# Splitting the first projections by tile and moving the last tiles' norm transposes behind their first pieces

## The reference

```python
xn = rms_norm(x, lp['norm_mix'])
proj = xn @ lp['w_in']                      # q | k | v | pool_in | two gates
q = rms_norm(q per head); k = rms_norm(k per head)
a = sliding-window attention (own 64-frame chunk and the two before, ALiBi bias, sink logit)
pl = pooling mixer: trailing means over 2/4/8/16 frames minus the frame, per-group map, scale
mix = (sigmoid(g0) * (a @ w_br_attn) + sigmoid(g1) * (pl @ w_br_pool)) @ w_out
x = x + mix
h = rms_norm(x, lp['norm_ffn']) @ lp['w_up']            # width 2 * 2816
hc = causal depthwise conv of width 3 over h
x = x + (gelu(gate half of hc) * value half of hc) @ w_down
```

## Time and profile before

| | |
|---|---|
| median of the timed runs | 4879.23 us (2 runs, 4861.53 and 4896.93) |
| profiled execution | 4373.59 us |
| its span, first to last instruction of the slowest core | 4372.1 us |
| spans of the 8 cores | 4332.4 to 4372.1 us |
| mean granted TensorE clock of the cores | 0.931 to 0.942 |
| TensorE, VectorE, ScalarE, GpSimd busy | 86%, 60%, 42%, 15% |

### The profile page before, as it was taken

One profiled execution on the slowest core, in us unless ns is written; L12 is line 12 of the kernel. 1 busy time (PEld: TensorE's weight loads), 2 busy tenths in 40 slices (PEclk: granted clock), 3 DMA queues, 4 the chain that ended last, 5 costly groups with the idle time before them and its releaser, 6 DMA issues.

```text
span 4372.1 us, 64992 instructions; the slowest of 8 cores (4332.4 to 4372.1 us)
## 1 busy us (share of the span) xinstructions
PE 3781.1 (86%) x21100; PEld 1882.6 (43%) x21100; DVE 2609.7 (60%) x4570; ACT 1837.1 (42%) x3723; POOL 640.3 (15%) x682
## 2 busy tenths in 40 slices
PE   3776479898898989898989989898989898989989
PEld 1434234443444444444444444444444444444444
DVE  2464547557474747566564746474757566574647
ACT  2333234344444535354444444353445344444443
POOL 1000000000121202020212112121202020211112
PEclk9877688899999999999999999999999999999999
DMA  7999967486333343343433433334334342443333
GB/s 132 196 195 180 192 152 206 117 184 181 130 134 114 130 150 131 105 145 126 158 105 138 139 138 124 121 139 145 122 117 146 125 154 96 149 127 138 114 125 120
DMA packets 104076, 616.74 MB, mean 141 GB/s; under 512 B 13600, under 2 KB 17728, under 8 KB 42304
## 3 DMA queue, kind: packets, MB, share of 16 engines
q1 hardware_dynamic: 88368, 528.69, 35.3%
q0 software_dynamic: 15376, 83.89, 12.7%
HBM read 621.11 MB, written 75.55 MB: 159 GB/s over the span
## 4 chain that ended last, share of the span: by engine, by line
PE 69%; DVE 14%; DMA 7%; issue 5%; ACT 4%; POOL 1%; DVEq 0%; SPq 0%; ACTq 0%; POOLq 0%
PE psb L885 27%; PE psb L940 13%; PE psb L790 11%; DVE srt L502 7%; DMA wslot<-wun 5%; PE psb L845 4%; PE psb L795 3%; PE psb L799 3%; PE psb L535 2%; PE psb L707 1%; ACT xh L453 1%; PE psb L713 1%; DMA wsc<-wslot 1%; PE psb L472 1%; DVE xsl L826 1%
## 5 line engine op out<-in xcount | busy, mean ns | idle before, releaser
L885 PE MATMUL psb<-xnT,wslot 128*128 128x512 bf16 (+5 forms) x6624 | 1365.7, 372 | 76.9 <-DMA wslot<-wun 35.9
L885 PEld LDWEIGHTS psb<-xnT,wslot 128*128 128x128 bf16 x6624 | 655.3, 103 | 783.2 <-issue 172.9
L940 PE MATMUL psb<-wslot,actT 128*128 128x512 bf16 (+1 forms) x2992 | 671.7, 386 | 35.0 <-DMA wslot<-wun 32.8
L908 POOL TENSOR_TENSOR actT<-ug,uv 128x512 bf16<-128x512 f32 x308 | 391.8, 1272 | 1092.4 <-DVE uv L903 756.1
L906 ACT ACTIVATE ug<-ug 128x512 f32<-128x512 f32 (+2 forms) x396 | 238.8, 603 | 682.7 <-DVE ug L903 682.5
L790 PE MATMUL psb<-xnT,wslot 128*128 128x512 bf16 (+2 forms) x2304 | 511.9, 378 | 5.9 <-DMA wslot<-wun 5.9
L940 PEld LDWEIGHTS psb<-wslot,actT 128*128 128x128 bf16 (+1 forms) x2992 | 294.2, 99 | 398.6 <-issue 78.4
L808 DVE TENSOR_TENSOR s0b<-psb,s0b 128x512 f32<-128x512 f32 (+2 forms) x144 | 94.5, 656 | 576.3 <-PE psb L799 569.9
L826 DVE TENSOR_TENSOR xsl<-psb,xsl 128x512 f32<-128x512 f32 (+1 forms) x396 | 270.4, 689 | 269.6 <-PE psb L940 209.8
L453 ACT ACTIVATE xh<-xsl 128x1024 bf16<-128x1024 f32 (+1 forms) x141 | 148.6, 1054 | 622.5 <-DVE xsl L826 340.3
L502 DVE RECIPROCAL srt<-srt 128x512 f32<-128x512 f32 (+1 forms) x108 | 353.1, 3269 | 91.1 <-ACT srt L500 90.3
(11 more groups left out here) (135 smaller groups left out, 3912.2 us busy)
## 6 DMA issues: line engine op xcount, KB each, us to landing
wslot<-wsc SPq DMA_DIRECT2D x366, 1024.0 KB, 6.0
wslot<-wun POOLq DMA_DIRECT2D x66, 1024.0 KB, 28.3
wsc<-wslot SPq DMA_DIRECT2D x48, 1024.0 KB, 13.9
wslot<-wsc SPq DMA_DIRECT2D x72, 512.0 KB, 6.6
xsl<-xp SPq DMA_DIRECT2D x35, 512.0 KB, 4.5
yp<-xsl SPq DMA_DIRECT2D x32, 512.0 KB, 5.0
...
```

Source lines behind the costliest of these rows:

```text
L885: S.op("pe", lambda e, k=k, bk=bk, half=half, pi=pi, wuv=wuv, c0=c0, c1=c1: e.matmul(out=psb[bk][:, c0:c1], lhsT=wuv[:, k, half * 256 + pi ...
L908: S.op("dve" if grp in groups[:2] else "pool", lambda e, ub=ub, j=j: e.tensor_tensor(out=actT[:, j, C0:N], in0=ug[ub][:, C0:N], in1=uv[ub] ...
L940: S.op("pe", lambda e, kc=kc, bk=bk, cs=cs, n=n, wdv=wdv, cb=cb, k0=k0, k1=k1: e.matmul(out=psb[bk][0:n, 0:512], lhsT=actT[:, kc, cs], rhs ...
```

## The change

norm_post of some tiles is no longer called where it was but put into a list, defer_q, and called from within the next stage.

- stage_F puts the last two of (at most three) tiles, 2 and 3 in a group of four, into the list. stage_G takes four banks at its start, for both j of the first weight unit with both halves, and runs the columns in three splits: tiles 0 and 1 (256 columns) in all four banks, then the transposes and the copy of tile 2, tile 2's columns (128) in all four banks, the transposes and the copy of tile 3, tile 3's columns (128) in all four.
- The last tile's norm_post before stage_B is put into the list in both layers. k_job takes both banks at once and runs the 384 columns of K 0 and K 1, then the transposes and the copy of the last tile, then its 128 columns for K 0; then follows the head norm's square for K 0, and K 1's 128 columns with the flush of the sum matmul come in the second job.

```diff
--- before.py
+++ after.py
@@ -460,6 +460,11 @@
                  reads=[xr, f"rstd{ti}"], writes=[f"xh{b}"])
 
         post_done = set()
+        defer_q = []
+
+        def run_deferred():
+            while defer_q:
+                defer_q.pop(0)()
 
         def norm_post(l, ni, t, ti):
             post_done.add((t["T"], l, ni))
@@ -527,14 +532,33 @@
             wkv, wkvr = W.get(U_KV)
             wkvv = wkv[:, 0:3072].rearrange("p (k c) -> p k c", k=8)
             npr = grp["np"]
+            kbanks = {}
+
+            def k_mm(g, c0, c1, rr):
+                bk = kbanks[g]
+                for k in range(8):
+                    S.op("pe", lambda e, g=g, k=k, bk=bk, c0=c0, c1=c1: e.matmul(out=psb[bk][:, c0:c1], lhsT=wkvv[:, k, g * 128:(g + 1) * 128],
+                                                                   rhs=xnT[:, k, c0:c1], start=(k == 0), stop=(k == 7)),
+                         reads=[wkvr] + rr, writes=[f"ps{bk}"])
+
             def k_job(g):
-                bk = pbank()
                 csp = tiles[-1]["col"]
-                for (c0, c1, rr) in ((0, csp, xres[:-1]), (csp, N, xres[-1:])):
-                    for k in range(8):
-                        S.op("pe", lambda e, g=g, k=k, bk=bk, c0=c0, c1=c1: e.matmul(out=psb[bk][:, c0:c1], lhsT=wkvv[:, k, g * 128:(g + 1) * 128],
-                                                                       rhs=xnT[:, k, c0:c1], start=(k == 0), stop=(k == 7)),
-                             reads=[wkvr] + rr, writes=[f"ps{bk}"])
+                if g == 0:
+                    kbanks[0] = pbank(); kbanks[1] = pbank()
+                    if defer_q:
+                        kbanks["split"] = True
+                        k_mm(0, 0, csp, xres[:-1])
+                        k_mm(1, 0, csp, xres[:-1])
+                        run_deferred()
+                        k_mm(0, csp, N, xres[-1:])
+                    else:
+                        k_mm(0, 0, N, xres)
+                else:
+                    if kbanks.get("split"):
+                        k_mm(1, csp, N, xres[-1:])
+                    else:
+                        k_mm(1, 0, N, xres)
+                bk = kbanks[g]
                 dests = [(0, npr * 128, kTw[0:64, 2 * g, 0:npr * 128], f"kTw{g}", (0, 64)),
                          (0, npr * 128, kTw[64:128, 2 * g + 1, 0:npr * 128], f"kTw{g}", (64, 128))]
                 for t in tiles:
@@ -641,6 +665,22 @@
                 return 128 if l == 0 else 256
             return 0
 
+        def col_splits(grp, C0):
+            act = [(ti, t) for ti, t in enumerate(grp["tiles"]) if t["col"] >= C0]
+            N_ = grp["N"]
+            if len(act) >= 3:
+                parts = [act[:-2], act[-2:-1], act[-1:]]
+            elif len(act) == 2:
+                parts = [act[:1], act[1:]]
+            else:
+                parts = [act]
+            out = []
+            for pi_, p in enumerate(parts):
+                c0 = p[0][1]["col"]
+                c1 = parts[pi_ + 1][0][1]["col"] if pi_ + 1 < len(parts) else N_
+                out.append((c0, c1, [f"xnT{ti}" for ti, _ in p]))
+            return out
+
         def prev_of(l, t):
             if t["kind"] == "s":
                 return (kcache[l], [f"kcache{l}"]), (Vcache[l], f"Vcache{l}"), (pinhist[l], f"pinhist{l}")
@@ -848,7 +888,11 @@
                         resid_add(grp, t, bk, cb)
                     norm_pre(l, 1, t, ti)
                 if 0 <= si - 2 < nt_:
-                    norm_post(l, 1, sub[si - 2][1], sub[si - 2][0])
+                    ndef = min(3, nt_) - 1
+                    if si - 2 >= nt_ - ndef:
+                        defer_q.append(lambda l=l, t=sub[si - 2][1], ti2=sub[si - 2][0]: norm_post(l, 1, t, ti2))
+                    else:
+                        norm_post(l, 1, sub[si - 2][1], sub[si - 2][0])
             W.done(U_OUT)
             W.done(U_OUT + 1)
 
@@ -870,22 +914,37 @@
                      reads=[f"corr{hid}", "ctmp"], writes=[f"corr{hid}"])
                 S.op("pool", lambda e, hs=hs, cr=cr: e.tensor_tensor(out=cr[:, :, 1], in0=hs[:, :, 1], in1=cw0, op=ALU.mult),
                      reads=[hr, "pv"], writes=[f"corr{hid}"])
+            pre_banks = {}
             for f in range(11):
                 wu, wur = W.get(U_UP + f)
                 wuv = wu[:].rearrange("p (k c) -> p k c", k=8)
-                for pi in range(2):
-                    j = 2 * f + pi
-                    ub = j % 2
-                    for half, (c, ubuf, ures) in enumerate(((j, ug[ub], f"ug{ub}"), (22 + j, uv[ub], f"uv{ub}"))):
-                        bk = pbank()
-                        csp = grp["tiles"][-1]["col"]
-                        splits = ((C0, csp, xres[:-1]), (csp, N, xres[-1:])) if (j == 0 and csp > C0) else ((C0, N, xres),)
-                        for (c0, c1, rr) in splits:
+                if f == 0:
+                    for pi in range(2):
+                        for half in range(2):
+                            pre_banks[(pi, half)] = pbank()
+                    for (c0, c1, rr) in col_splits(grp, C0):
+                        for (pi, half), bk in pre_banks.items():
                             for k in range(8):
                                 S.op("pe", lambda e, k=k, bk=bk, half=half, pi=pi, wuv=wuv, c0=c0, c1=c1: e.matmul(
                                     out=psb[bk][:, c0:c1], lhsT=wuv[:, k, half * 256 + pi * 128: half * 256 + (pi + 1) * 128],
                                     rhs=xnT[:, k, c0:c1], start=(k == 0), stop=(k == 7)),
                                     reads=[wur] + rr, writes=[f"ps{bk}"])
+                        if defer_q:
+                            defer_q.pop(0)()
+                    run_deferred()
+                for pi in range(2):
+                    j = 2 * f + pi
+                    ub = j % 2
+                    for half, (c, ubuf, ures) in enumerate(((j, ug[ub], f"ug{ub}"), (22 + j, uv[ub], f"uv{ub}"))):
+                        if f == 0:
+                            bk = pre_banks[(pi, half)]
+                        else:
+                            bk = pbank()
+                            for k in range(8):
+                                S.op("pe", lambda e, k=k, bk=bk, half=half, pi=pi, wuv=wuv: e.matmul(
+                                    out=psb[bk][:, C0:N], lhsT=wuv[:, k, half * 256 + pi * 128: half * 256 + (pi + 1) * 128],
+                                    rhs=xnT[:, k, C0:N], start=(k == 0), stop=(k == 7)),
+                                    reads=[wur] + xres, writes=[f"ps{bk}"])
                         S.op("act", lambda e, bk=bk, c=c, ubuf=ubuf: e.activation(out=ubuf[:, C0:N], in_=psb[bk][:, C0:N], func=ACTF.Identity,
                                                                                  bias=pvc(l, OFF_CB + c, 1), scale=pvc(l, OFF_CW[2] + c, 1)),
                              reads=[f"ps{bk}", "pv"], writes=[ures])
@@ -985,7 +1044,10 @@
                         norm_pre(l, 0, t, ti)
                 for ti, t in enumerate(grp["tiles"]):
                     if (t["T"], l, 0) not in post_done:
-                        norm_post(l, 0, t, ti)
+                        if ti == len(grp["tiles"]) - 1 and ti > 0:
+                            defer_q.append(lambda l=l, t=t, ti=ti: norm_post(l, 0, t, ti))
+                        else:
+                            norm_post(l, 0, t, ti)
                 if DEBUG_STOP == "A":
                     break
                 stage_B(l, grp, W)
```

## The result

| | before | after |
|---|---|---|
| median of the timed runs | 4376.88 us | 4451.69 us |
| ratio to before | | 1.0226, 95% interval 1.0165 to 1.0288 |
| profiled execution | 4373.6 us | 4449.3 us |
| spans of the cores | 4332.4 to 4372.1 us | 4429.1 to 4447.8 us |

The change makes the kernel slower by 2.3%, about 98 us. That it is slower is shown; whether by more than the 2% that counts here is not, since the interval reaches from 1.7% to 2.9%. The ratios compare only executions in which no half of the chip's cores had a clearly lower granted clock (the kernel before took 4350.2 us with all its cores at 0.94, and 4861.1 us with four of them at 0.81), while the medians take all, which is why they differ by 75 us and not by 98. Over ten runs the kernel before has a median of 4376.9 us, near its profile, and not the 4879.2 us of the two timed runs on which the forecast stood.

A forecast was written before the change was run, and what follows sets the result against it. The prediction took TensorE (86% busy) as the bound, with at most 176 us of its waits on offer; seam and group terms summed to +74 us, on the timed median 4879.23 giving 4953 us (+1.5%), range 4880 to 5010 us.

The forecast's parts named there:

- the sum: Total of all terms, 50 + 18 - 12 + 18 = +74 us, added to the timed median 4879.23 us.
- Up-projection seam: Output projection to up-projection, 14 times in groups 2 to 8: two exposed copies, +3.6 us each, 50 us.
- K seam before layer 1: Down-projection to K projection, 8 times: first sum matmul L498 comes later, +2.2 us each, 18 us.
- K seam before layer 0: Down-projection to K projection, 8 times: cover exists, L498 comes earlier, -1.5 us each, -12 us.
- The drain of VectorE after the stage: After the up-projection: VectorE's late finish is hidden by the down-projection, whose first half is over 20 us of matmuls.
- the slack of 4.8: End of the up-projection: TensorE's last bank is released 4.8 us early, against a loss of 3.2, so no new wait.
- Group 1: Up-projection with L908's product on VectorE: the 8.5 us later start passes through, less at layer 0; 6 us each.
- The rest of a pass: From the first L498 to the end of the output projection, both layers: forecast 0.
- Rival 1: Whole kernel: xh waits vanish and copies stay covered; about 4740 us, -2.8%; chance 0.06.
- Rival 2: Whole kernel: gains and losses at the seams cancel, nothing to measure; 4883 us, +0.1%; chance 0.17.
- Rival 3: Up-projection: VectorE becomes the bound, or waits of 1.74 us lower the clock; 5006 us, +2.6%; chance 0.17.

The follow-up runs named there:

- e6: The changed kernel with each deferred tile's transposes one split earlier in the up-projection; ratio to the kernel before 1.0035, a steady group 472.2 to 473.3 us.
- e4: The kernel before with only the K seam before layer 0 changed; ratio 1.0125 (0.9925 to 1.0324), a steady group 471.1 to 471.2 us.
- e3: The kernel before, nothing deferred, only the first up-projection weight unit filled in three splits over four banks; ratio 0.9961, a steady group 471.1 to 471.7 us.
- e10: The changed kernel with group 1's up-projection product on GpSimd, not VectorE; ratio to the kernel before 1.0146, group 1 484 to 492 us.
- e8: The changed kernel with VectorE's copy ahead of rstd, transposes one split earlier, and the last tile's between the 384-column K pieces; ratio to the kernel before 0.9794.

## Why the prediction was right and wrong

**The time, 4953 us, was wrong, and the step that failed is in the sum: "The timed runs of before are longer, 4861.5 and 4896.9, median 4879.23, 11.6% over the profile", and then "so I add the 74 us as they are: 4953 us".** In its place the runs showed that the kernel before stands at 4376.9 us (median of ten), so the level was 502 us too high, while the changed kernel came at 4451.7. The level came from two runs that disagreed with the profile by 11.6%, and I took them for the truth where the profile had the granted clock beside it. Nothing in the argument explained the 11.6%; an unexplained gap of that size should have widened the range down to the profile's level. Why these two runs were at that level stays open: their clocks are not on record.

**That the profile's 4373.6 + 74 = 4448 is near the 4451.7 is luck.** The slowest core of that profile, core 7, was some 22 us longer than the slowest of cores 0 to 5 (4372.1 against 4350.4 us), 16 us of it in group 1, where it stood at 0.81. That hid the 24 us by which the change costs more than the sum says.

**The size of the change: +74 forecast, about +98 measured, 1.5% against 2.3%.** By terms:

- Up-projection seam, 3.6 each: 3.7 and 3.1. Right, also in its parts: first piece 1.1 us earlier, two copies exposed, shown by e6, which takes them away and gets back 8 us a group.
- K seam before layer 1, +2.2: 2.3, and the waits changed from xh to xnT as written.
- K seam before layer 0, -1.5: -1.3, and e4 shows that nothing of it reaches the end.
- "The drain of VectorE after the stage is hidden by the down-projection" was wrong for layer 1, +1.3 us each, 9 us. The term stood at nothing. I had looked for a bank wait inside the stage (there is none in the steady groups, as forecast) and not at the residual adds and the next group's transposes behind it. e3 shows it with the bank fill alone. VectorE's lag behind TensorE at the end of the stage grew by 3.9 us (8.4 to 12.3), not by 3.2, and stayed inside the slack of 4.8.
- Group 1, "6 each, between 3.6 and 8.5": the up-projection grew by about 8 in each layer, near the upper end, 18 us for the group and not 13. e10 shows that VectorE is the cause. The words "at layer 0 less" rest on a misreading: I had read core 7, whose clock was 0.81 in that stage, and found no wait for VectorE there, but core 5, at its full clock, has one of 5.5 us in 8 waits in layer 0 and 4.7 in 7 in layer 1 (L885 on ug of L900).
- The rest of a pass, 0: +1.4 us a group, 10 us, between L498 and the end of the output projection. In layer 0 TensorE's waits for qT grow from 2.1 to 2.7 us a pass to 3.5 to 3.9; in layer 1 they shrink by 0.5 to 1.2 us, but the time at half clock grows from 8.0 us a pass to 11 to 13. No run isolates either.

**The rivals.** Rival 1 is half right in a way I did not see: the xh waits did shrink by 135 us, and with VectorE's order put right and the transposes one piece ahead the idea is worth having (e8). I had written that tile 1's copy is late itself, but priced its removal nowhere. Rival 2 did not come. Rival 3's loss came near (2.3% against its 2.6%) by another way: neither of its two mechanisms is there in the steady groups. No row of L944 waiting for VectorE stands in the list of groups 2 to 8, and across the waits of 1.48 us in the seam of group 2, layer 1, the granted clock stayed at 1.00 from 1440 to 1446 us. The Trainium skill, "TensorE: Matmul & The Clock Gate", section "A second HAM failure mode: psum-queue depth-cycling", tells of micro-idles between groups of matmuls that make the clock oscillate in another kernel; two waits of 1.48 us a seam did not do it here. Where the section "Back-to-back issue gap" of the same page of the Trainium skill has 81 ns per matmul of 128 columns, this kernel took 56 ns, the changed one too.
